# A two-layer diffusion backbone on one core: modulation passes placed anew, identity products in TensorE's waits, an earlier token copy and earlier expert loads

## The chip, the core and the metric

The kernel runs on one core of a Trainium2 chip. The metric is the device time of one execution in microseconds, as the median of several runs. All tensors are fp32. The engines are called by the names of the profile: PE (TensorE), DVE (VectorE), ACT (ScalarE), POOL (GpSimd) and SP (SyncE, which only issues transfers here).

## What is computed

Two layers (DEPTH 2) over 256 latent tokens and 256 context tokens of width 1024. The second layer returns the latent tokens only, so it works on half of the queries. Cut to what matters:

```python
for l in range(2):
    mod  = silu(c)     @ w_mod[l] + b_mod[l]      # 6 x 1024: shift, scale, gate, twice
    modc = silu(c_ctx) @ w_mod[l] + b_mod[l]      # the same for the context tokens
    h = rms_norm(x, norm1_g) * (1 + s1) + sh1     # hc likewise, with modc
    z = h @ w_in                                  # 1024 x 6144: four mixers and 4 x 1024 gates
    ya = differential_attention(z)                # "A": 4 heads of 32, two softmaxes
    yb = hyena_long_convolution(z)                # "B"
    yc = windowed_gqa(z)                          # "C": 4 heads of 64, 2 of keys
    yd = conformer_convolution(z)                 # "D"
    y  = sum(sigmoid(z_gate_i + b_gate_i) * (y_i @ w_branch[i]) for i in range(4)) @ w_out
    x  = x + g1 * y
    t  = rms_norm(x, norm2_g) * (1 + s2) + sh2
    x  = x + g2 * hier_moe(t)     # top group of 4, top 2 of its 4 experts: 16 experts of 1024x512
```

## The kernel before

Nothing in the order of work is left to a scheduler. `layer_order(l)` writes one list of steps, each a pair of an engine letter (T is PE, V is DVE, S is ACT, P is POOL) and a name such as `("br", 1, 2, 7)`. Each engine runs its own steps in the order of that list and waits on semaphores for the steps of others. `merge` and `spread` distribute one list evenly over another. The step names used below:

- `gate` (line 1163) is the product of the normed tokens with one eighth of a branch's gate columns, 16 PE instructions; `br` (line 1264) is a branch's output product. ACT, DVE and POOL turn both into the gated sum. The gates are the filler with which PE bridges the attentions' waits.
- Attention A is `qkTA` (line 1271), `sA` (1285), maxima on DVE (2398), exponentials on ACT (1800), `pTA` (1300) turned out by ACT (1810), `yA` (1311), its norm `yM` (1319), DVE's `yrA` and `ynA` (2441) and `yR` (1326). Attention C has `qkTC`, `sC` and `yC` (1278, 1293, 1336). `rsA` on DVE follows `ssA`, sums of squares (2364), and stands ahead of the rotation (2083 to 2103).
- `modv` (line 2180) is the adaLN modulation as DVE work: passes of 128x1024 over chunks of `wmod`. 120 of them are strewn over the stages, one column group (l, ch) at a time; 8 passes a group in layer 0, and 4 or 8 in layer 1. Two groups per layer run on PE instead (line 1116).
- `wo` (line 1347) is the output projection; then `xup` (2455, 2457), the second norm (`rstd`, `scale` at 2210, transposes at 1137), the router's logits (1366, 1372), `hb` (1377), `modB` (1129), `rank` (1385 to 1390), `slots`, `list` (1397) and, in layer 0, `sidelist` (1404), which build the lists of tokens of each expert. `rows` (2560 to 2584) works out row numbers for the later gathers.
- The experts run in pairs: tokens gathered by POOL (1975), turned on PE (1444, and 1449 for the side expert), copied out by DVE (2595, 2601), then up and gate products (1456, 1458) and down products (1466). In layer 1 the first tokens are made by a product (1578) instead of a gather.
- Between the layers stand `mod` and `modT` (1116, 1122) and the `mix` products (1356, 1357), which wait for the gathered expert results.

SP loads the weights in order of first use into a ring of six places of 1 MB (`plan_ring`, line 1064), and waits, ahead of a load, for the last reader of what lay there. Expert matrices are 2 MB and take two places; some go to buffers of other stages that are free by then (`load_early`, line 946, and lines 995, 1010, 1016), and later ones into places that the expert loop frees (957, 959). SP is one queue: a load behind one that waits is late too.

PSUM has 8 banks, which `plan_banks` gives out in rotation.

## Time and profile before

| | before |
|---|---|
| median of 3 runs | 1573.72 us (1573.6 to 1573.95) |
| the profiled execution | 1572.35 us, span 1570.6 us |
| PE busy | 1457.3 us, 93% of the span |
| DVE / ACT / POOL busy | 48% / 18% / 7% |
| chain that ended last | PE 79%, DVE 11%, DMA 3%, issue 3%, SP's queue 2%, ACT 2% |
| moved | 355.57 MB, mean 226 GB/s |
| granted PE clock, mean | 0.971 |

### The profile page before, as it was taken

The page shows a single profiled execution, that of the slowest core. Times are in us where ns is not written, and L with a number is a line of the kernel's source. Part 1 is how long each engine was busy: PE and PEld are TensorE (multiplying, and loading weights), DVE is VectorE, ACT ScalarE, POOL GpSimd, SP SyncE. Part 2 cuts the span into 40 slices and gives each one's busy share as a digit, 9 for nine tenths or more (in the row PEclk, how much of TensorE's full clock was granted, in tenths as well). Part 3 has the DMA queues.
Part 4 walks back from the last instruction along what each step waited for, and adds up shares of the span by engine and source line. Part 5 has one row for each costly group of instructions (what it writes and reads, how often), then busy time and mean ns, then how long its engine had stood idle before and what let it go on. Part 6 is the DMA issues. An engine that isn't in the chain of part 4 may idle for free.

```text
span 1570.6 us, 17267 instructions
## 1 busy us (share of the span) xinstructions
PE 1457.3 (93%) x6306; PEld 737.0 (47%) x6306; DVE 753.8 (48%) x1740; ACT 279.8 (18%) x579; POOL 114.0 (7%) x107
## 2 busy tenths in 40 slices
PE   6999999988899999699999998999879997999987
PEld 2544644443444444533333334865767874433332
DVE  4297676684565876511221214685887214211112
ACT  3201011421331200311111101111232202000000
POOL 0000011000111210000000001001001110000000
PEclk8999999998999999899999999999999998999999
DMA  9520243211324432799999976326534327999996
GB/s 374 198 79 31 77 158 137 81 54 53 108 81 145 174 142 68 294 351 405 415 407 418 409 318 258 138 81 240 219 123 168 114 75 311 424 418 422 422 421 244
DMA packets 49330, 355.57 MB, mean 226 GB/s; under 512 B 5568, under 2 KB 5952, under 8 KB 21984
## 3 DMA queue, kind: packets, MB, share of 16 engines
q1 hardware_dynamic: 41936, 330.79, 53.6%
q0 software_dynamic: 4016, 14.24, 2.4%
q10 hardware_dynamic: 3296, 9.44, 1.6%
q8 instruction: 53, 0.87, 0.2%
q14 instruction: 29, 0.24, 0.0%
HBM read 343.88 MB, written 10.56 MB: 226 GB/s over the span
## 4 chain that ended last, share of the span: by engine, by line
PE 79%; DVE 11%; DMA 3%; issue 3%; SPq 2%; ACT 2%; POOL 0%; DVEq 0%; ACTq 0%; POOLq 0%
PE ps L1163 25%; PE ps L1456 19%; PE ps L1176 6%; PE ps L1466 5%; PE ps L1347 5%; PE ps L1264 4%; SPq L946 2%; DVE n_ L2267 2%; DMA hT<-w 2%; PE ps L1137 1%; PE ps L1478 1%; DMA ring<-wmod 1%; PE ps L1300 1%; DVE mx L2398 1%; PE ps L1285 1%
## 5 line engine op out<-in xcount | busy, mean ns | idle before, releaser
L1163 PE MATMUL ps<-hT,ring 128*128 128x512 f32 (+1 forms) x1344 | 458.9, 497 | 4.5 <-ACT n_ L1800 3.0
L1163 PEld LDWEIGHTS ps<-hT,ring 128*128 128x128 f32 x1344 | 258.6, 195 | 180.2 <-issue 155.4
L1456 PE MATMUL ps<-ring,m 128*64 128x512 f32 x624 | 279.6, 600 | 10.3 <-ACT m L1883 3.5
L1456 PEld LDWEIGHTS ps<-ring,m 128*64 128x64 f32 x624 | 82.5, 138 | 184.7 <-issue 175.0
L2180 DVE SCALAR_TENSOR_TENSOR spare<-ring,crow 128x1024 bf16<-128x1024 f32 x120 | 154.1, 1284 | 4.1
L1176 PE MATMUL ps<-ring,hT 128*128 128x512 f32 (+1 forms) x352 | 125.1, 515 | 0.0
L1458 PE MATMUL ps<-n_,m 128*64 128x512 f32 x224 | 102.5, 607 | 0.0
L1264 PE MATMUL ps<-yT,ring 128*128 128x512 f32 (+1 forms) x256 | 95.9, 498 | 0.0
L1458 PE MATMUL ps<-wide,m 128*64 128x512 f32 x208 | 93.7, 597 | 0.0
L1176 PEld LDWEIGHTS ps<-ring,hT 128*128 128x128 f32 x352 | 66.7, 190 | 55.1 <-issue 51.4
L1458 PE MATMUL ps<-hT,m 128*64 128x512 f32 x208 | 91.9, 595 | 0.0
L1947 POOL TENSOR_TENSOR wide<-wide,gates 128x512 f32<-128x512 f32 (+1 forms) x48 | 61.8, 1287 | 411.9 <-DVE gates L2357 411.9
L1347 PE MATMUL ps<-ring,wide 128*128 128x512 f32 x192 | 83.1, 593 | 1.1 <-issue 1.1
L1759 ACT ACTIVATE gates<-ps,hbg 128x512 f32<-128x512 f32 (+1 forms) x64 | 37.1, 580 | 245.1 <-PE ps L1163 183.4
L2605 DVE SCALAR_TENSOR_TENSOR m<-m,ps 128x512 f32<-128x512 f32 x16 | 11.0, 687 | 142.9 <-ACT m L1869 142.9
L2267 DVE SCALAR_TENSOR_TENSOR n_<-n_,col 128x512 f32<-128x512 f32 (+1 forms) x120 | 74.2, 618 | 4.3
L2357 DVE SCALAR_TENSOR_TENSOR gates<-gates,ps 128x512 f32<-128x512 f32 (+1 forms) x48 | 26.6, 554 | 97.5 <-PE ps L1264 92.2
L2618 DVE TENSOR_TENSOR m<-m,ps 128x512 f32<-128x512 f32 x16 | 11.0, 687 | 106.0 <-PE ps L1458 106.0
L1264 PEld LDWEIGHTS ps<-yT,ring 128*128 128x128 f32 x256 | 46.1, 191 | 30.9 <-issue 24.8
L1466 PE MATMUL ps<-ring,yT 128*32 128x512 f32 x256 | 58.1, 595 | 0.0
L1347 PEld LDWEIGHTS ps<-ring,wide 128*128 128x128 f32 x192 | 36.2, 190 | 46.1 <-issue 46.1
L1975 POOL DMA_INDIRECT m<-h_scratch,m x15 | 14.2, 946 | 484.5 <-PE ps L1444 335.0
(362 smaller groups left out, 1710.9 us busy)
## 6 DMA issues: line engine op xcount, KB each, us to landing
ring<-w SPq DMA_DIRECT2D x39, 2048.0 KB, 11.4
ring<-win SPq DMA_DIRECT2D x52, 1024.0 KB, 5.1
ring<-wmod SPq DMA_DIRECT2D x48, 1024.0 KB, 5.1
n_<-w SPq DMA_DIRECT2D x13, 2048.0 KB
hT<-w SPq DMA_DIRECT2D x13, 2048.0 KB, 18.1
wide<-w SPq DMA_DIRECT2D x13, 2048.0 KB, 15.9
ring<-wbr SPq DMA_DIRECT2D x8, 1024.0 KB, 5.0
ring<-wout SPq DMA_DIRECT2D x8, 1024.0 KB, 5.1
```

Of the source, the lines that this page charges most:

```text
L946: sp.dma_start(ap, fourths(experts_weights[w][1, 2 * e + two][:, 512 * k:512 * (k + n)]))\
L1163: last = pe.matmul(b[:, 0:W], w[:, k, jj * P:(jj + 1) * P], hT[:, k, 0:W], start=(k == 0), stop=(k == KD - 1))
L1176: last = pe.matmul(b[:, 0:wid], hT[:, k, t * P:(t + 1) * P], chunk3(parts[k // ks], ks)[:, k % ks, 0:wid], start=(k == 0), stop=(k == KD - 1))
L1264: last = pe.matmul(b[:, 0:W], w[:, k, j * P:(j + 1) * P], yT[:, bi in (1, 2), k, 0:W], start=(k == 0), stop=(k == 1))
L1347: last = pe.matmul(b, acc[:, k, t * P:(t + 1) * P], chunk3(part_of, 4)[:, k % 4, :], start=(k == 0), stop=(k == KD - 1))
L1456: pe.matmul(ps[0:HALF, bnk, :], left[:, k, 0:HALF], even[k], start=(k == 0), stop=(k == n_k - 1), skip_group_check=True)
L1458: last = pe.matmul(ps[HALF:P, bnk, :], left[:, k, HALF:P], odd[k], start=(k == 0), stop=(k == n_k - 1), skip_group_check=True)
L1466: last = pe.matmul(ps[SIDE * g:SIDE * (g + 1), bnk, :], left[:, k0 + k, rows_:rows_ + SIDE], weights[:, k0 + k, cols_], start=(k == 0), st ...
L1759: last = act.activation(gth[:, g % 2, 0:W], bank(("gate", l, bi, j))[:, 0:W], ACT.Tanh, bias=hbg[:, bi * 8 + j:bi * 8 + j + 1], scale=0.5)
L1947: last = nc.gpsimd.tensor_tensor(acc[:, j, 0:W], acc[:, j, 0:W], gtmp[:, g % 2, 0:W], ALU.add)
L2180: last = v.scalar_tensor_tensor(out=spare[:, 0, :].bitcast(BF16), in0=chunk3(cn, 2)[:, block_ % 2, :], scalar=0.5, in1=crow[:, s, :], op0= ...
L2267: last = v.scalar_tensor_tensor(out=o, in0=ud[:, j, 0:ns, k:k + 256], scalar=w(k), in1=o, op0=ALU.mult, op1=ALU.add)
```

## The change

- **DVE's modulation passes.** In layer 0 group (0, 7) goes from attention A to attention C, and the groups behind it each move one stage on; three groups instead of two stand in the `wo` stage, four passes behind each of its first half tiles, and none behind the last two. In layer 1 groups 8 and 9 go from the conformer and rope stage to attention C, and 10 and 11 from attention A to the first half of the last gates. Ahead of each attention A, none stands behind the last three tiles of `zA`.
- **Identity products.** `busy` steps multiply the identity by itself, 128x128 by 128x512, into a bank that nobody reads: in layer 0 two ahead of `rank`, one behind `list`, three behind `sidelist`, and after the experts two ahead of `mod` and four ahead of the `mix`; in layer 1 five ahead of the second norm's last tile, three ahead of `rank` and one behind `list`.
- **Order in the router.** `modB` moves behind `rank`. In layer 0 the first copies of turned tokens (`firstturned`) move ahead of `rows`.
- **Loads.** `wout` comes in chunks of 2 MB that take two places. In layer 1, 4 MB of expert weights (`n_`, `m`, `con`, `mr`) are issued behind the last `yC`, ahead of the last gate weights and of `wout`; 4 MB more (`yT` and others, and the ring's `w1`) behind `br(1,2,7)`, where they stood behind the first `wo`.

```diff
@@ -258,6 +258,11 @@
     return net, spectrum
 
 
+def kept_busy(l, where, n):
+
+    return [("T", ("busy", l, where, n))] if n else []
+
+
 def norm_steps(l, n, tiles):
 
     out = [("S", ("sq", l, n, t)) for t in tiles]
@@ -352,15 +357,15 @@
 
     turned = lambda chunks: [[g] for c in chunks for g in modv_steps(*c)]
     if l == 0:
-        with_za, with_conformer, in_a, in_c = [(0, 4)], [(0, 5), (0, 6)], [(0, 7)], [(0, 8), (0, 9)]
-        behind, with_wo = [(0, 10), (0, 11), (1, 0), (1, 1)], [(1, 2), (1, 3)]
+        with_za, with_conformer, in_c = [(0, 4)], [(0, 5), (0, 6)], [(0, 7), (0, 8)]
+        behind, with_wo = [(0, 9), (0, 10), (0, 11), (1, 0)], [(1, 1), (1, 2), (1, 3)]
     else:
-        with_za, with_conformer, in_a, in_c, behind, with_wo = [(1, 6), (1, 7)], [(1, 8), (1, 9)], [(1, 10), (1, 11)], [], [], []
+        with_za, with_conformer, in_c, behind, with_wo = [(1, 6), (1, 7)], [], [(1, 8), (1, 9)], [(1, 10), (1, 11)], []
     za_groups = []
     for t in range(TILES):
         za_groups += [[("T", ("zAq", l, t)), ("S", ("zAqout", l, t))]] if t < tt else []
         za_groups += [[("T", ("zAk", l, t)), ("S", ("zAkout", l, t)), ("P", ("sqA", l, t)), ("V", ("ssA", l, t))]]
-    o += merge(za_groups, turned(with_za)) + [("V", ("rsA", l))]
+    o += merge(za_groups[:-3], turned(with_za)) + [s for g in za_groups[-3:] for s in g] + [("V", ("rsA", l))]
     projections = [[("P", ("sqC", l, t)), ("V", ("ssC", l, t))] for t in range(TILES)]
 
     def prepared(b):
@@ -402,12 +407,14 @@
     half = len(units) // 2
     turns = [g for g in prepared("C") if g[0][0] == "T"]
     ropes = [[("V", ("rsC", l))]] + [g for g in prepared("C") if g[0][0] == "V"]
-    o += settled(spread(conformer[12:] + spread(gate_groups(1, False), turned(in_a)),
+    o += settled(spread(conformer[12:] + gate_groups(1, False),
                         units[:half] + spread(units[half:], ropes) + turns))
     o += settled(spread(spread(gate_groups(0, False), turned(in_c)), attention("C")))
     net, spectrum = filter_groups(l + 1) if l + 1 < DEPTH else ([], [])
 
-    o += merge(spread(gate_groups(2, False), turned(behind)), net)
+    last_gates = gate_groups(2, False)
+    n = len(last_gates) if l == 0 else len(last_gates) // 2
+    o += merge(spread(last_gates[:n], turned(behind)) + last_gates[n:], net)
     o += gate_steps(l, (4, 5))
     for t in range(tt):
         for hf in range(2):
@@ -419,32 +426,39 @@
                 o += [("S", ("sq", l, 2, u)) for u in range(t)] + [("V", ("rstd", l, 2, 0, t))]
             o += [("V", ("xup", l, t, hf))]
             n, left = 2 * t + hf, turned(with_wo)
-            o += [s for g in left[n * len(left) // (2 * tt):(n + 1) * len(left) // (2 * tt)] for s in g]
+            o += [s for g in left[4 * n:4 * n + 4] for s in g]
     o += [g[0] for g in spectrum[1:]]
     o += [("V", ("scale", l, 2, t)) for t in range(tt - 1)]
     normed = norm_steps(l, 2, [tt - 1])
+    o += kept_busy(l, "norm", 0 if with_side(l) else 5)
     o += normed[:1] + [g[1] for g in spectrum[1:]] + normed[1:] + modulated_steps(l, 2)
     o += [("T", ("lg", l)), ("S", ("lgrow", l)), ("T", ("lgT", l)), ("V", ("lgout", l)), ("V", ("picks", l))]
     for t in range(tt):
         for hf in range(2):
             o += [("T", ("hb", l, t, hf)), ("S", ("hbout", l, t, hf))]
         o += [("S", ("hstore", l, t))]
-    o += gate_steps(l, (10, 11))
-    o += [("T", ("rank", l)), ("V", ("slots", l))]
+    o += kept_busy(l, "rank", 2 if with_side(l) else 3)
+    o += [("T", ("rank", l)), ("V", ("slots", l))] + gate_steps(l, (10, 11))
     if not with_side(l):
         o += [("V", ("firstrows", l))]
     o += [("T", ("list", l)), ("V", ("list", l))]
+    o += kept_busy(l, "list", 1)
     if with_side(l):
         o += [("V", ("sideslots", l)), ("T", ("sidelist", l)), ("V", ("sidelist", l))]
+        o += kept_busy(l, "sidelist", 3)
     o += [("V", ("weights1", l)), ("S", ("rexp", l)), ("V", ("weights2", l))]
     if not with_side(l):
         o += [("V", ("weighted", l))]
+    if with_side(l):
+        o += [("V", ("firstturned", l))]
     o += [("V", ("rows", l))]
     o += [("T", ("experts", l)), ("S", ("experts", l)), ("V", ("experts", l)), ("P", ("experts", l))]
     o += [("V", ("diag", l))] if with_side(l) else []
     if l + 1 < DEPTH:
         one, two = mod_steps(l + 1, [4]), mod_steps(l + 1, [5])
+        o += kept_busy(l, "boundary", 2)
         o += one[:2] + two[:2] + one[2:] + two[2:]
+        o += kept_busy(l, "gather", 4)
     if l + 1 < DEPTH:
         return o + boundary_steps(l)
     for t in range(tt):
@@ -474,7 +488,7 @@
     if kind == "br":
         return [("wbr", l, rest[0])]
     if kind == "wo":
-        return [("wout", l, rest[1], half) for half in range(2)]
+        return [("wout", l, rest[1])]
     if kind == "experts":
 
         return [("w1", l), ("w3", l), ("w2", l)]
@@ -488,7 +502,7 @@
 
 def places_of(chunk):
 
-    return 2 if chunk[0] in ("w1", "w3", "w2") else 1
+    return 2 if chunk[0] in ("w1", "w3", "w2", "wout") else 1
 
 
 def plan_ring():
@@ -521,6 +535,10 @@
 
 CHUNKS, PLACE, BEFORE = plan_ring()
 CHUNK_AT = {name: i for i, (name, _) in enumerate(CHUNKS)}
+ORDER_AT = {s: i for i, s in enumerate(ORDER)}
+BEHIND_SCORES = next(i for i, (name, _) in enumerate(CHUNKS) if name[1] == DEPTH - 1 and any(
+    ORDER_AT[CHUNKS[b][1]] > ORDER_AT["T", ("yC", DEPTH - 1, live(DEPTH - 1) - 1)] for b in BEFORE[i]))
+LAST_WOUT = ("wout", DEPTH - 1, 1)
 FIRST_WIN = {l: next(name for name, _ in CHUNKS if name[:2] == ("win", l)) for l in range(DEPTH)}
 
 
...
@@ -975,6 +995,10 @@
             sp.dma_start(col[:], cols).then_inc(params_landed, 16)
             sp.dma_start(row[:], rows).then_inc(params_landed, 16)
             for i, (name, _) in enumerate(CHUNKS):
+                if i == BEHIND_SCORES:
+                    sp.wait_ge(tensor_done, tensor("yC", 1, live(1) - 1))
+                    sp.dma_start(odd_at["w1"], w1[1, 1]).then_inc(odd_landed["w1"], 16)
+                    load_early(("w3", 0), ("w3", 1, 0), "attention")
                 for b in BEFORE[i]:
 
                     old, (engine, last) = CHUNKS[b]
@@ -990,15 +1014,9 @@
                     base = l * PAIRS
                     weights = experts_weights[name[0]]
                     sp.dma_start(place, weights[l, 0]).then_inc(here, 16)
-                    if name[0] == "w1":
+                    if name[0] == "w1" and not l:
                         sp.wait_ge(tensor_done, tensor("yC", l, live(l) - 1))
                         sp.dma_start(odd_at["w1"], w1[l, 1]).then_inc(odd_landed["w1"], 16)
-                        if l:
-                            load_early(("w3", 0), ("w3", 1, 0), "attention")
-                            sp.wait_ge(tensor_done, tensor("br", l, 2, KD - 1))
-                            sp.wait_ge(vector_done, vector(*mod_ready(l, 11)))
-                            load_early(("w1", 1), ("w1", 1, 1), "branches")
-                            load_early(("w3", 1), ("w3", 1, 1), "branches")
                     if name[0] != "w2":
                         continue
                     if l:
@@ -1057,11 +1075,16 @@
                 if name == FIRST_WIN[1]:
 
                     sp.wait_ge(y_gathered[live(0) - 1], 32)
-                if name[0] in ("wmod", "wout"):
+                if name[0] == "wmod":
                     src = source[name[0]][name[1], name[2]][:, PLACE_COLS * name[3]:PLACE_COLS * (name[3] + 1)]
                 else:
                     src = source[name[0]][name[1], name[2]]
                 sp.dma_start(place, src).then_inc(here, 16)
+                if name == LAST_WOUT:
+                    sp.wait_ge(tensor_done, tensor("br", 1, 2, KD - 1))
+                    sp.wait_ge(vector_done, vector(*mod_ready(1, 11)))
+                    load_early(("w1", 1), ("w1", 1, 1), "branches")
+                    load_early(("w3", 1), ("w3", 1, 1), "branches")
                 if name == ("wmod", 0, 0, 1):
                     sp.dma_start(x[:], xin).then_inc(x_landed, 16)
                 if name == ("wmod", 0, 2, 1):
@@ -1120,6 +1143,11 @@
                     pe.wait_ge(scalar_done, scalar("modrow", l, *rest))
                     for j in range(4):
                         last = pe.transpose(b[:, j * P:(j + 1) * P], mr[:, rest[0] % 2, j * P:(j + 1) * P], ident)
+                    last.then_inc(tensor_done, 1)
+                elif kind == "busy":
+                    _, n_products = rest
+                    for i in range(n_products):
+                        last = pe.matmul(b, ident, ident.unsqueeze(1).broadcast_to([P, 4, P]), start=True, stop=True)
                     last.then_inc(tensor_done, 1)
                 elif kind == "modB":
                     ch, v = rest
...
@@ -2556,6 +2595,10 @@
                     link(v.scalar_tensor_tensor(out=pw[:, 0, 0:tt], in0=p2, scalar=0.5, in1=total, op0=ALU.mult, op1=ALU.mult))
                     last = v.tensor_tensor(pw[:, 1, 0:tt], pw[:, 0, 0:tt], rtmp[:, 9, 0:tt], ALU.mult)
                     last.then_inc(vector_done, 1)
+                elif kind == "firstturned":
+                    turned(l, 0)
+                    side_turned_out(0)
+                    v.nop().then_inc(vector_done, 1)
                 elif kind == "rows":
                     link(v.tensor_copy(tok, c("token")))
```

What stands in DVE's row in layer 1's attention A before: maxima (2398), softmax weights (2420 to 2423), rotation of C (2083 to 2103), a gate (2357), and two passes (2180).

```order
L2180 SCALAR_TENSOR_TENSOR spare,mod<-ring,crow 128x1024
L2398 TENSOR_REDUCE mx<-ps 128x1 x2
L2399 TENSOR_SCALAR nm<-mx 128x2
L2420 RECIPROCAL rr<-sums 128x2
L2421 TENSOR_TENSOR nlam<-rr,nlam 128x1
L2422 TENSOR_SCALAR n_<-n_,rr 128x512
L2423 SCALAR_TENSOR_TENSOR n_<-n_,nlam 128x512
L2083 TENSOR_TENSOR m<-m,rsc 128x128
L2085 TENSOR_TENSOR m<-m,row 128x128
L2096 TENSOR_TENSOR n_<-m,con 128x128
L2100 TENSOR_TENSOR n_<-m,con 128x4x16 x2
L2103 TENSOR_TENSOR m<-n_ 128x128
```

The same place of the change; its line numbers are 39 higher (2437 for 2398, 2122 for 2083, and a pass would be 2219).

```order
L2437 TENSOR_REDUCE mx<-ps 128x1 x2
L2438 TENSOR_SCALAR nm<-mx 128x2
L2459 RECIPROCAL rr<-sums 128x2
L2460 TENSOR_TENSOR nlam<-rr,nlam 128x1
L2461 TENSOR_SCALAR n_<-n_,rr 128x512
L2462 SCALAR_TENSOR_TENSOR n_<-n_,nlam 128x512
L2122 TENSOR_TENSOR m<-m,rsc 128x128
L2124 TENSOR_TENSOR m<-m,row 128x128
L2135 TENSOR_TENSOR n_<-m,con 128x128
L2139 TENSOR_TENSOR n_<-m,con 128x4x16 x2
L2142 TENSOR_TENSOR m<-n_ 128x128
L2486 SCALAR_TENSOR_TENSOR yT<-n_,col,ps 128x2x128
```

The passes before the maxima and behind the branch product are gone; the first one that follows stands behind attention C's first maxima.

PE's row in layer 0's router before: `hb` (1377), `modB` (1129), `rank` (1385 to 1390), `list` (1397), `sidelist` (1404) and the turning of the tokens (1444).

```order
L1377 MATMUL ps<-con,hT 128x128 x32
L1129 MATMUL ps<-con,mod 128x128 x16
L1385 MATMUL ps<-m,con 128x80
L1388 MATMUL ps<-m,con 128x48
L1388 MATMUL ps<-m,con 128x32
L1388 MATMUL ps<-m,con 128x16
L1390 MATMUL ps<-m,con 128x80
L1397 MATMUL ps<-m 128x16 x8
L1404 MATMUL ps<-m 64x16 x8
L1444 MATMUL ps<-con,m 128x128 x8
```

The same place of the change, with the identity products at line 1150 and `modB` at 1157.

```order
L1404 MATMUL ps<-con,hT 128x128 x32
L1150 MATMUL ps<-con 128x512 x2
L1412 MATMUL ps<-m,con 128x80
L1415 MATMUL ps<-m,con 128x48
L1415 MATMUL ps<-m,con 128x32
L1415 MATMUL ps<-m,con 128x16
L1417 MATMUL ps<-m,con 128x80
L1157 MATMUL ps<-con,mod 128x128 x16
L1424 MATMUL ps<-m 128x16 x8
L1150 MATMUL ps<-con 128x512
L1431 MATMUL ps<-m 64x16 x8
L1150 MATMUL ps<-con 128x512 x3
```

The two identity products stand where `modB` stood, `modB` is behind `rank`, and three products lie between `sidelist` and the turning of the gathered tokens.

SP's queue in layer 1 before, from the last gate weights (`win`) to the early expert loads.

```order
L1064 DMA ring<-win 128x2048 x3
L1064 DMA ring<-wout 128x2048 x4
L992 DMA ring<-w 128x4096
L995 DMA n_<-w 128x4096
L946 DMA m<-w 128x1536
L946 DMA con<-w 128x1024
L946 DMA con<-w 128x512
L946 DMA m<-w 128x512
L946 DMA mr<-w 128x512
```

The same loads of the change (line 1000 for 995, 966 for 946, 1082 for 1064).

```order
L1082 DMA ring<-wmod 128x2048
L1000 DMA n_<-w 128x4096
L966 DMA m<-w 128x1536
L966 DMA con<-w 128x1024
L966 DMA con<-w 128x512
L966 DMA m<-w 128x512
L966 DMA mr<-w 128x512
L1082 DMA ring<-wmod 128x2048
L1082 DMA ring<-win 128x2048 x2
L1082 DMA ring<-wout 128x4096 x2
L966 DMA yT<-w 128x2048
```

Six expert loads, 4 MB, now stand ahead of the last `wmod` chunk, of the last two `win` chunks and of `wout`.

## Rows read from the trace of the kernel before

**Rows 1.** First line of the profile page: the span.

```profile
span 1570.6 us, 17267 instructions
```

**Rows 2.** Windows: PE, PEld, DVE, ACT, POOL busy us (instructions), PEclk, DMA share, GB/s.

```profile
300.00:402.00 102.00, 88.86 (x314) 43.60 (x312) 67.52 (x197) 25.25 (x69) 10.07 (x7) 0.93 0.21 73
1098.00:1202.00 104.00, 88.90 (x461) 72.39 (x459) 83.93 (x212) 27.96 (x67) 9.69 (x10) 0.92 0.47 172
1202.00:1246.00 44.00, 43.13 (x251) 34.60 (x252) 20.95 (x64) 16.63 (x41) 5.78 (x8) 1.00 0.37 135
1246.00:1282.00 36.00, 36.00 (x180) 31.59 (x175) 3.39 (x9) 4.17 (x9) 5.06 (x7) 1.00 0.34 119
...
1350.00:1560.00 210.00, 197.56 (x882) 71.78 (x878) 25.56 (x47) 17.18 (x30) 5.62 (x6) 1.00 0.98 405
```

**Rows 3.** Windows of line 2180 alone: DVE busy us (instructions), PEclk, DMA share.

```profile
300.00:402.00 102.00, 9.87 (x16) 0.93 0.21 73
1098.00:1202.00 104.00, 19.97 (x32) 0.92 0.47 172
```

**Rows 4.** Timeline of PE, layer 0, attention A.

```profile
335.58 7.03 PE L1163 MATMUL ps<-hT,ring 128*128 128x512 f32 x16
...
350.72 9.23 PE L1163 MATMUL ps<-hT,ring 128*128 128x512 f32 x16
...
388.51 0.41 PE L1326 MATMUL ps<-con,n_ 128*128 128x128 f32 x2 [2.92 <-DVE n_ L2441]
```

**Rows 5.** Timeline of PE, layer 1, attention A.

```profile
1103.39 1.09 PE L1271 MATMUL ps<-con,m 128*128 128x128 f32 x4 [4.92 <-DVE m L2103]
1104.28 6.12 PE L1163 MATMUL ps<-hT,ring 128*128 128x256 f32 x16
...
1111.54 3.62 PE L1163 MATMUL ps<-hT,ring 128*128 128x256 f32 x16
```

**Rows 6.** Timeline of DVE ahead of layer 1's attention A.

```profile
1091.86 1.57 DVE L2180 SCALAR_TENSOR_TENSOR spare<-ring,crow 128x1024 bf16<-128x1024 f32 x1
...
1095.29 0.19 DVE L2379 TENSOR_SCALAR small<-ssa 128x64 f32<-128x64 f32 x1
```

**Rows 7.** Timeline of PE, layer 0, norm 2 and router.

```profile
633.11 6.74 PE L1137 MATMUL ps<-n_,x 128*128 128x128 f32 x58 [2.14 <-DVE n_ L2210]
...
662.13 1.94 PE L1444 MATMUL ps<-con,m 128*128 128x128 f32 x8 [2.62 <-DMA m<-h_scratch,m]
664.01 1.11 PE L1449 MATMUL ps<-con,yT 64*128 64x64 f32 x8
667.44 1.11 PE L1456 MATMUL ps<-ring,m 128*64 128x512 f32 x1 [2.32 <-DVE m L2595]
```

**Rows 8.** Timeline of DVE, layer 0, end of the router.

```profile
661.82 0.17 DVE L2560 CAST m<-con 128x4 uint32<-128x4 f32 x1
...
666.70 0.69 DVE L2595 COPY m<-ps 128x512 f32<-128x512 f32 x1
```

**Rows 9.** Windows: the same columns as in rows 2, end of layer 0's router.

```profile
660.00:670.00 10.00, 5.54 (x22) 3.26 (x24) 6.56 (x33) 0.91 (x3) 2.77 (x3) 0.50 0.68 252
```

**Rows 10.** Timeline of PE between the layers.

```profile
958.39 1.30 PE L1356 MATMUL ps<-wide,n_ 128*128 128x512 f32 x2 [3.44 <-DMA hT<-y_scratch,m]
```

**Rows 11.** Timeline of PE, layer 1, norm 2 and first tokens.

```profile
1316.13 5.90 PE L1137 MATMUL ps<-n_,x 128*128 128x128 f32 x30 [3.07 <-DVE n_ L2210]
...
1335.53 6.63 PE L1578 MATMUL ps<-m,wide 128*128 128x128 f32 x32 [1.08 <-DVE m L2526]
```

**Rows 12.** Timeline of DVE, layer 1, copy of the first tokens.

```profile
1342.25 0.69 DVE L2595 COPY m<-ps 128x512 f32<-128x512 f32 x1 [1.84 <-PE ps L1578]
```

**Rows 13.** Timeline of SP's queue, layer 1: expert loads and the first refill.

```profile
1303.83 0.33 SPq L992 DMA_DIRECT2D ring<-w  x1
...
1350.13 0.33 SPq L959 DMA_DIRECT2D ring<-w  x1
```

**Rows 14.** Timeline of PE, layer 1's experts.

```profile
1503.33 0.61 PE L1456 MATMUL ps<-x,m 128*64 128x512 f32 x1 [3.05 <-DMA gates<-w]
```

More of the change, by code:

```diff
@@ L1343, in _ @@
                     pe.wait_ge(pool_done, pool("gadd", l, 2, KD - 1))
+                    use(("wout", l, half))
+                    w = chunk3(("wout", l, half))
                     for k in range(KD):
-                        part_of = ("wout", l, half, k // 4)
-                        use(part_of)
-                        last = pe.matmul(b, acc[:, k, t * P:(t + 1) * P], chunk3(part_of, 4)[:, k % 4, :],
-                                         start=(k == 0), stop=(k == KD - 1))
+                        last = pe.matmul(b, acc[:, k, t * P:(t + 1) * P], w[:, k, :], start=(k == 0), stop=(k == KD - 1))
                     last.then_inc(tensor_done, 1)
@@ L2672, in pair @@
                             side_result(e)
-                    turned(0)
-                    if side:
-                        side_turned_out(0)
-                    else:
+                    if not side:
+                        turned(l, 0)
                         v.wait_ge(rows_weighed, 1)
```

24 lines of the change are left out of this document (13 added, 11 removed).

## Prediction

> **What bounds the kernel.** The page first: the span is 1570.6 us [rows 1], and the profiled execution took 1572.35 us, 1.4 us less than the median of the runs. PE is busy 93% of the span, so the gain must come from PE's idle time or from the clock that it is granted. The windows say where both lie. In layer 0's attention A PE works 88.86 of 102.00 us at a granted clock of 0.93, in layer 1's 88.90 of 104.00 at 0.92, while DVE is busy for 67.52 and 83.93 us; the 44 us behind it (attention C) hold only 0.9 us of idle PE, and the last gates (1246 to 1282) none at all: 36.00 of 36.00 us at full clock, DVE busy 3.39 us [rows 2]. Layer 1's experts move 405 GB/s at a DMA share of 0.98 [rows 2]: there the transfers set the pace, and PE is seen waiting for one for 3.05 us [rows 14]. The timelines of PE and DVE then say what ends each wait.
>
> **Attention A, layer 0.** PE waits 13.1 us (102.00 less 88.86). Behind each longer wait it runs at half speed for a while: the same 16 gate instructions take 7.03 us when it was busy and 9.23 us behind a wait [rows 4]. A mean of 0.93 [rows 2] means 14% of 102 us at the lower of the two levels (1.2 and not 2.4 GHz), some 14 us, which costs at most half of it, 7.1 us; I take 6. So 19 us are at stake. The change takes 8 passes out, 9.87 us of DVE time [rows 3]. They are no sum to subtract: a pass of 1.2 us costs only where it stands ahead of a maximum, a softmax weight or the norm `ynA`, for which PE waits (2.92 us [rows 4]). More gates also go into the waits for `yR`. The ends: 3 us if only a third of the passes stood on the path, 17 if nearly all waits and their clock go. Some latencies (exponentials on ACT, turning on ACT) stay without passes. I take **8**.
>
> **Attention A, layer 1.** PE waits 15.1 us and the clock of 0.92 costs at most 8.3, of which I take 6 (a group of 16 gates took 6.12 us behind the wait of 4.92 us, and 3.62 later [rows 5]). Out go 16 passes, 19.97 us of DVE's 83.93 [rows 2, 3]; DVE is nearer to being the bound here than in layer 0. Ahead of it, two passes stood between the last `ssA` and `rsA`: from 1091.86 to 1095.29, 3.4 us [rows 6], on the path to the 4.92 us wait on DVE [rows 5]. These 3.4 us come in nearly whole. Together **13**, between 6 and 20.
>
> **Where the passes go.** In layer 1, 8 go to attention C: 10 us more on a DVE busy 20.95 of 44 us beside a PE without idle time [rows 2]: cost 1, between 0 and 3, the upper end if three passes stand right ahead of a maximum. 8 go to the last gates, 10 us on a DVE busy 3.39 of 36: nothing, since PE's gates cover them; without that cover each costs 1.25 us (19.97 through 16 [rows 3]). In layer 0 eight more stand in the `wo` stage ahead of the last two half tiles, under output products: nothing. Behind the last two `xup` none is left, where one pair (2.5 us by the same price) held DVE ahead of the wait of 2.14 us [rows 7]: gain **2**, between 0 and 2.6.
>
> **Start of layer 0's experts.** Tokens are turned by 664.07 and the side tokens by 665.12, but DVE works on `rows` from 661.82 on and copies only at 666.70; PE starts at 667.44 after 2.32 us [rows 7, 8]. With the copy first, it is done in 0.7 us from 664.1, and PE starts as its turning ends at 665.1: 2.3 us. `rows` then runs under the first products. The clock in this window is 0.50 [rows 9]: turning at 1.94 us for 8 would take about half, of which 0.9 us are on the path, and the first five steps of the experts (1.11 against about half) would give 2.5 us if PE was kept at 2.4 GHz. An identity product is two instructions of 128x512, as a gate is 16: 7.03 through 16 makes 0.44 each [rows 4], so 0.88 us a product, and 1.76 at the lower level. Three behind `sidelist` end 2.6 to 5.3 us after it, while PE waited for the gathered tokens 2.62 us and more: warm they fit, cold they hold up the turning by up to 2.5 us. Sum **5**, between -2.5 and 6.5. The Trainium skill bears on this ("TensorE: Matmul & The Clock Gate", Part 4): a transpose in PE's transpose mode does not count as PE-busy in the same way and does not engage the full clock. By that rule the turning itself would lose again what the identity products kept, and the sum here would be 2.5 less. The trace shows 58 norm transposes in 6.74 us in layer 0 and 30 in 5.90 us in layer 1 [rows 7, 11], so transposes run at either level; what sets the level no row decides. I give the 2.5 us less a chance of 0.4, within this term's bounds.
>
> **Between the layers.** Six products, 5.3 us at full clock, in waits of 2.4 us ahead of `mod` and 3.44 us ahead of the `mix` [rows 10]. The four ahead of the `mix` take 3.5 us warm: they end when the transfer lands or up to 1.7 us later, since the two ahead of `mod` run cold. The first `mix` products then run warm, 1.8 us less. **0**, between -3 and +1.
>
> **Layer 1, norm 2 and router.** Thirty transposes took 5.90 us behind a wait of 3.07, against 58 in 6.74 in layer 0 [rows 7, 11]: warm they take 3.5, but are paced by DVE's copies, so 1.8. The first tokens' product, 6.63 us at a low clock [rows 11], would take some 3.7; its copy at 1342.25 waited 1.84 us for it [rows 12], and DVE's own work ahead of the copy limits the gain to these 1.8. With 0.4 for `modB` in the wait for `slots`: **4**, between 1 and 5.
>
> **Loads in layer 1.** SP came to the expert weights at 1303.83 [rows 13], after a stretch in which nothing moved. From 1350.13, the first refill, the schedule still asks for 38 matrices of 2.097 MB and 7 gathers of 0.524 MB: 83.4 MB. The window from 1350 moved 405 times 210, 85.0 MB [rows 2]. So only 1.6 MB of the early loads was still owed at the first refill: 3.9 us at 413 GB/s (405 through 0.98). Loading 8 MB earlier brings at most that much to the experts, which stay bound by DMA; it gives **3.8**, between 0 and 7, the upper end if all PE waits such as [rows 14] go. What is won before the experts is kept, because the refills start with PE's first expert, not by the clock.
>
> The loads have a price ahead of them. 4.2 MB go into SP's queue before the last `wmod`, two `win` chunks and `wout`. One branch's gates are eight channels in 36 us [rows 2], 4.5 us each, and a `win` chunk serves two. The third of the stage, the first one behind the expert loads, is needed 18 us after `yC`. Ahead of it are 4.2 MB of expert weights and up to 5 MB of ring chunks, estimated: 9.2 MB at 0.413 MB/us are 22 us, from a start some 4 us before `yC`'s end. It lands at 18 us, so on the edge: I take a stall of **-2**, between -5 and 0. The Trainium skill says ("DMA: Bandwidth & Descriptors", Queues, rings and completion order) that SP's transfers share one ring on each of the 16 engines, consumed in ring order. By that rule none of the later chunks overtakes; without it the gate weights would share the bandwidth and the stall would still be 2 to 5. The trace's windows do not show the two side by side.
>
> **Sum.** 8 + 13 - 1 + 2 + 5 + 0 + 4 + 3.8 - 2 = 32.8 us. 1572.35 - 32.8 = 1539.6, and 1.4 more for the median: **1541 us**.
>
> **Rivals.**
> (a) The passes carry their stall along (0.20). In attention C or the last gates they delay `ropeC`'s, `mxC`'s or the gates' own DVE work, and the waits in attention A were latency of the chain DVE, ACT, PE, not passes. For it: 8 of 16 passes go into a stage where PE waits for maxima; part of A's waits name ACT. Against it: PE has 0.9 us of idle in C, DVE half of its time [rows 2]. Both attentions then give only 5 and C costs 3: 18 less, **1559 us**.
> (b) Identity products on the path (0.06), the other side. 21 products cost 0.88 us each warm and 1.76 cold, 18 to 37 us, if PE's waits were not there, because the releaser itself waits for PE (banks in rotation, `modB` behind `rank`). It becomes slower than before only from where more than 33 us are lost, so every product must run cold and in the way, or half of them beside (a): **1578 us**. Against it: waits of 2.32, 2.62, 3.07 and 3.44 us end on DVE or on a transfer [rows 7, 10, 11].
> (c) SP's queue starves the last gates (0.06): all of the 9.2 MB late and `wout` behind it too, 10 us of stall (4.2 MB through 0.413) in place of 2: **1549 us**, inside the forecast's range.
> (d) Nearly all waits go (0.13): 17 and 20 in the attentions and 7 in the experts: 19 more, **1522 us**; I expect from it half at most, 1530.
> The forecast itself has 0.55, with 1532 to 1552 as its own range.
>
> **How the numbers follow.** What a measurement of this kernel can tell from no change is about 0.2%, 3.1 us. The range of 8 in 10 takes in (c), half of (d) and most of (a): 1526 to 1561. Faster: the forecast, (c), (d) and (a), but for the tail of (a) in which the experts' early loads give nothing either: 0.91. Within 0.2%: 0.04. Slower: 0.05, of (b).
>
> **What the changed profile would show.** Right: idle PE in the two attentions under 10 us each and a clock above 0.95; no pass between the last `ssA` and `rsA`; the first copy of turned tokens ahead of `rows` in layer 0, and PE's first expert product within 1 us of the turning; the window of the router's end well above 0.50; PE's wait for a transfer in the last gates under 3 us; layer 1's experts shorter by 4 us from the first refill on. Wrong: waits on `win` of over 5 us in the last gates, maxima of C late behind passes, identity products that end after the step behind them was ready, or a token turning that still runs at half speed.

## The result and the profile after

The changed kernel takes 1557.19 us in the median of 6 runs (1554.92 to 1561.74), against 1573.12 us before. The ratio is 0.9904, 95% interval 0.9893 to 0.9916: 16 us faster, where 33 were forecast. As a time it lies inside the prediction's range of 1526 to 1561; the gain is about half of the forecast one. Its runs spread over 6.8 us; the six of the kernel before spread over 1.6, and its runs beside the experiments over 3.1, 5.7 and 4.9. The profiled execution is one of the slower ones: 1559.5 us, span 1557.8 us.

The first line of the changed kernel's page, and the page's row of the modulation passes:

```profile
span 1557.8 us, 17344 instructions
...
L2219 DVE SCALAR_TENSOR_TENSOR spare<-ring,crow 128x1024 bf16<-128x1024 f32 x120 | 155.3, 1295 | 9.0 <-DMA ring<-wmod 4.9
```

The passes take what they took, 1.3 us each; ahead of them DVE now stands idle for 9.0 us in all, 4.9 of them for `wmod` chunks.

The changed kernel's windows (PE, PEld, DVE, ACT, POOL busy, clock, DMA share, GB/s): both attentions A, ten microseconds at a time in the last gates of layer 1, the experts of layer 1 and the end of layer 0's router.

```profile
300.00:402.00 102.00, 88.48 (x317) 42.51 (x317) 56.32 (x179) 25.21 (x70) 10.36 (x8) 0.93 0.15 52
1098.00:1202.00 104.00, 96.16 (x507) 76.57 (x506) 64.64 (x183) 33.17 (x81) 10.98 (x13) 0.97 0.32 112
1235.00:1245.00 10.00, 10.00 (x49) 8.79 (x48) 6.73 (x11) 1.42 (x3) 3.39 (x2) 1.00 1.01 423
1245.00:1255.00 10.00, 5.00 (x22) 4.10 (x21) 4.80 (x9) 0.47 (x1) 3.11 (x2) 0.92 1.04 424
1255.00:1265.00 10.00, 10.00 (x37) 8.28 (x35) 0.72 (x2) 0.47 (x1) 1.00 (x2) 0.74 0.47 195
1350.00:1550.00 200.00, 190.17 (x830) 68.89 (x827) 23.34 (x43) 16.10 (x28) 4.68 (x5) 0.99 0.95 393
660.00:670.00 10.00, 9.78 (x61) 3.98 (x63) 5.53 (x26) 1.19 (x2) 1.84 (x2) 1.00 0.92 355
```

Read against [rows 2], the first row is the surprise: DVE has 11 us less to do in layer 0's attention A, and PE's 13.5 us of idle time and its clock of 0.93 are what they were. The last row is the opposite case: the clock of 0.50 [rows 9] is now 1.00. The windows of the last gates show a PE idle for 5 us beside a DMA share of 1.04, where it had no idle time before.

Windows at fixed times cut shifted stages at different places, so the rest goes by milestones on PE's timeline, the first or the last row of a line. Stages that are alike in both are left out. Lengths in us:

| stage, from PE's timeline | before | changed | forecast gain | gain |
|---|---|---|---|---|
| layer 0, A's turned queries to C's first scores | 178.9 | 177.9 | 8 | 1.0 |
| layer 0, C's first scores to last `yC` | 90.1 | 88.4 | 0 | 1.7 |
| layer 0, first `wo` to the norm's last transposes | 71.6 | 70.1 | 2 | 1.5 |
| layer 0, `rank` to the end of the up products | 292.0 | 287.8 | 5 | 4.3 |
| from there to the last `mix` between the layers | 31.1 | 29.8 | 0 | 1.3 |
| from there to layer 1's turned queries | 130.2 | 127.7 | 3.4, in the 13 | 2.5 |
| layer 1, turned queries to C's first scores | 98.6 | 95.2 | 9.6, in the 13 | 3.3 |
| layer 1, C's first scores to last `yC` | 44.6 | 44.9 | -1 | -0.3 |
| layer 1, last `yC` to first `wo` | 36.3 | 44.5 | -2 | -8.2 |
| layer 1, end of `wo` to the first expert product | 32.4 | 27.3 | 4 | 5.1 |
| layer 1, first to last up product | 217.4 | 216.4 | 3.8 | 1.0 |

These gains and 0.4 us lost ahead of the first stage are 12.8 us, as the spans have it (1570.6 less 1557.8).

The last gates on the changed kernel's PE timeline:

```profile
1244.77 3.62 PE L1191 MATMUL ps<-hT,ring 128*128 128x256 f32 x16
1248.23 1.03 PE L1292 MATMUL ps<-yT,ring 128*128 128x256 f32 x4
1254.25 6.59 PE L1191 MATMUL ps<-hT,ring 128*128 128x256 f32 x16 [5.00 <-issue]
1260.68 1.03 PE L1292 MATMUL ps<-yT,ring 128*128 128x256 f32 x4
```

The wait is named "issue", a wait for nothing that the profile names; SP's queue and the load's time to landing say what it was.

```profile
1231.07 0.33 SPq L1082 DMA_DIRECT2D ring<-wmod  x1
1231.82 0.33 SPq L1000 DMA_DIRECT2D n_<-w  x1
...
1235.58 0.45 SPq L966 DMA_DIRECT2D mr<-w  x1
1238.22 0.33 SPq L1082 DMA_DIRECT2D ring<-wmod  x1
1239.79 4.05 SPq L1082 DMA_DIRECT2D ring<-win  x2
```

The DMA view of 1215 to 1280 on the `win` chunks, where 13.1 is the median of three, and that of 1239.6 to 1240.2, which holds the one issued at 1239.79 alone:

```profile
ring<-win SPq DMA_DIRECT2D x3, 1024.0 KB, 13.1
ring<-win SPq DMA_DIRECT2D x1, 1024.0 KB, 14.4
```

In the median of the whole kernel a `win` chunk lands 4.9 us after its issue; this one took 14.4, and 1239.79 plus 14.4 is 1254.2, when PE's stall ends. After it the same gates take 6.59 us and not 3.62. So the stall cost 5.0 and the clock another 3.0.

### The profile page after: what moved, and what is told of

Read it like the earlier page. It is cut to its first block and busy times, and to the rows that moved or that the text cites. A ratio compares the mean times of both kernels' runs of the same rounds, so it can differ in the third digit from the quotient of the medians.

```text
span 1557.8 us, 17344 instructions
## 1 busy us (share of the span) xinstructions
PE 1464.1 (94%) x6348; PEld 733.9 (47%) x6348; DVE 756.3 (49%) x1740; ACT 279.8 (18%) x579; POOL 119.0 (8%) x107
## 5 line engine op out<-in xcount | busy, mean ns | idle before, releaser
L1974 POOL TENSOR_TENSOR wide<-wide,gates 128x512 f32<-128x512 f32 (+1 forms) x48 | 69.7, 1452 | 407.7 <-DVE gates L2396 407.7
```

The lines of the kernel that those rows point to most:

```text
L1974: last = nc.gpsimd.tensor_tensor(acc[:, j, 0:W], acc[:, j, 0:W], gtmp[:, g % 2, 0:W], ALU.add)
```

## The experiments

**1 and 2. Where the loads stand.** The changed kernel, with the first 4 MB of the expert loads behind the last gate weights (the first edit, below), or with the code of the early loads as it was before the change (the second), where all of them stand behind `wout`:

```diff
-BEHIND_SCORES = next(i for i, (name, _) in enumerate(CHUNKS) if name[1] == DEPTH - 1 and any(
-    ORDER_AT[CHUNKS[b][1]] > ORDER_AT["T", ("yC", DEPTH - 1, live(DEPTH - 1) - 1)] for b in BEFORE[i]))
+BEHIND_SCORES = next(i for i, (name, _) in enumerate(CHUNKS) if name == ("wout", DEPTH - 1, 0))
```

> The changed kernel with the first group of early expert loads (4.2 MB) issued behind the last gate weights and ahead of the output weights. Theory Q (the queue starves the gates): the 44.5 us from the end of layer 1's last yC to the first output product come back to 36 to 37 us, PE's wait of 5.0 us inside the last gates and the half-speed product behind it are gone, and nothing is lost elsewhere, since the expert loads still land before layer 1's experts: 7 to 8 us faster than the changed kernel, about 1549 us. Rival D (DVE and the passes moved into the last gates hold them up): the stage stays at 43 to 45 us and the time at 1557.

> The changed kernel with all early expert loads back behind the first output product, as before. Theory Q: the last gates take 36 to 37 us (8 us won), but layer 1's experts owe the transfers again what the early loads brought. If the experts are bound by transfers as I priced it, they give back 3 to 4 us: about 1553 us. If the early loads are worth nothing there: 1549 us. If they are worth all that they move (8 MB, 19 us): 1568 us.

Measured: 1551.02 us (ratio 0.986, 0.9845 to 0.9875) and 1553.86 us (0.9882, 0.9866 to 0.9897). In both the last gates take 36.3 us again. PE's timeline of experiment 1 in that stage has no wait until the first `wo`:

```profile
1249.51 3.62 PE L1190 MATMUL ps<-hT,ring 128*128 128x256 f32 x16
1252.96 1.03 PE L1291 MATMUL ps<-yT,ring 128*128 128x256 f32 x4
1253.82 3.62 PE L1190 MATMUL ps<-hT,ring 128*128 128x256 f32 x16
...
1268.53 1.96 PE L1374 MATMUL ps<-ring,wide 128*128 128x512 f32 x4 [0.72 <-issue]
```

In experiment 1 the `win` chunk issued at 1240.20 landed after 7.0 us. The queue was the cause. Both kernels have the passes in that stage too, and it takes what it took before the change, so they cost nothing there.

Experiment 2 is not as late as the kernel before. Its `wout` still comes in chunks of 2 MB, and SP comes to the expert loads at 1267.05, 64 us ahead of the first refill; before the change it was 46 us, and it is 87 in experiment 1 and 107 in the changed kernel. From the first refill (1331.61 and 1331.48) to the last product that waits for a matrix (1513.71 and 1512.78) experiments 1 and 2 take 182.1 and 181.3 us; it was 183.3 before, and 180.6 in the changed kernel. So 4 MB moved by 23 us did not lengthen this stretch. Whether the 2.8 us between the two medians are more than the spread stays open; their intervals overlap. In the two profiles the second kernel is longer at two places at which only the clock differs, by 1.7 us each: layer 0's attention C, and the products behind the last wait for a matrix, of which the last section tells.

**3. No identity products.**

```diff
-    return [("T", ("busy", l, where, n))] if n else []
+    return [("T", ("busy", l, where, n))] if n and (False) else []
```

> The changed kernel without any identity product. If they hold the clock up as I priced them, it loses some 2.5 us at the start of layer 0's experts, 1.8 in layer 1's norm, 2 to 3 in layer 1's first tokens and gets about 1 us back between the layers: 5 to 8 us slower than the changed kernel, about 1564 us. Rival: the order alone (modB, the token copy) gives the gain and the products are idle work: within 2 us of the changed kernel, or faster by up to 3.

Measured: 1568.07 us in 8 runs (ratio 0.9974, 0.9963 to 0.9984), 11 us slower than the changed kernel, where I had expected 5 to 8. The stages that hold such products give 8.8 us of it: `rank` to the end of layer 0's up products 289.8 and not 287.8 us, up products to last `mix` 31.2 and not 29.8, end of layer 1's `wo` to its first expert product 32.7 and not 27.3. The experts of layer 1 are 1.0 longer. Stages without these products differ too: layer 1's attention A by 0.6 and layer 0's attention C by 1.7 longer, layer 0's attention A by 1.4 shorter. Without them, at the end of layer 0's router, PE's timeline reads:

```profile
658.14 1.94 PE L1471 MATMUL ps<-con,m 128*128 128x128 f32 x8 [2.66 <-DMA m<-h_scratch,m]
660.22 1.11 PE L1476 MATMUL ps<-con,yT 64*128 64x64 f32 x8
661.27 1.11 PE L1483 MATMUL ps<-ring,m 128*64 128x512 f32 x1
```

And in the changed kernel:

```profile
655.42 4.79 PE L1150 MATMUL ps<-con 128*128 128x512 f32 x6
660.05 1.04 PE L1471 MATMUL ps<-con,m 128*128 128x128 f32 x8
661.02 0.71 PE L1476 MATMUL ps<-con,yT 64*128 64x64 f32 x8
661.94 0.64 PE L1483 MATMUL ps<-ring,m 128*64 128x512 f32 x1 [0.22 <-DVE m L2091]
```

Three products, two PE instructions each, began at the low clock and took 4.79 us, and the turning comes 1.9 us later for them. Behind them everything runs at the high clock, and the up products are 2.6 us shorter in all.

**4. Layer 0's attention A in its old order, without the passes.** The passes are put in where they stood, so that the gates fall as before, and are then left out of the stage:

```diff
+    marks = turned([(0, 7)] if l == 0 else [(1, 10), (1, 11)])
+    if l == 0:
+        stage = settled(spread(conformer[12:] + spread(gate_groups(1, False), marks),
+                               units[:half] + spread(units[half:], ropes) + turns))
+        o += [s for s in stage if s[1][0] != "modv" or s[1][2] not in (7,)]
...
```

> The changed kernel, with every engine's order in layer 0's attention A as it was before the change but without the eight modulation passes, which stay where the change put them. Theory O (the passes were worth something, but taking them out of the list shifted the gates away from PE's waits, which cost as much): the stage from the first turned queries of A to the first scores of C gets 3 to 8 us shorter than in the changed kernel and than before, total 1549 to 1554. Rival P (the passes never stood on the path; the waits are latency of scores, softmax and turning): the stage is as long as before within 1.5 us and the total stays at 1556 to 1558.

Measured: 1557.91 us (0.9908, 0.9893 to 0.9923), the changed kernel's time; but the stage takes 172.8 us, 5.1 less. The changed kernel's PE timeline at the first two `yR` (L1354), the second with the next turning of softmax weights (L1328) close behind:

```profile
304.41 0.66 PE L1354 MATMUL ps<-con,n_ 128*128 128x128 f32 x2 [3.55 <-DVE n_ L2480]
...
330.63 0.42 PE L1328 MATMUL ps<-con,m 128*128 128x128 f32 x2
330.88 1.88 PE L1292 MATMUL ps<-yT,ring 128*128 128x512 f32 x4
333.70 0.41 PE L1354 MATMUL ps<-con,n_ 128*128 128x128 f32 x2 [0.93 <-DVE n_ L2480]
339.45 0.69 PE L1328 MATMUL ps<-con,n_ 128*128 128x128 f32 x2 [5.35 <-ACT m L1827]
```

In the old order a gate group stands between `yM` and `yR` at both places, and `yR` (L1360 in this experiment) waits for nothing:

```profile
301.27 7.03 PE L1197 MATMUL ps<-hT,ring 128*128 128x512 f32 x16
308.14 0.38 PE L1360 MATMUL ps<-con,n_ 128*128 128x128 f32 x2
...
324.73 7.03 PE L1197 MATMUL ps<-hT,ring 128*128 128x512 f32 x16
331.59 0.38 PE L1360 MATMUL ps<-con,n_ 128*128 128x128 f32 x2
```

The longest waits that this experiment keeps there, without any pass in the stage:

```profile
345.72 1.09 PE L1345 MATMUL ps<-n_,m 128*64 128x128 f32 x16 [1.63 <-ACT n_ L1843]
...
360.67 8.74 PE L1197 MATMUL ps<-hT,ring 128*128 128x512 f32 x16 [3.04 <-ACT n_ L1833]
...
383.81 0.41 PE L1360 MATMUL ps<-con,n_ 128*128 128x128 f32 x2 [2.92 <-DVE n_ L2486]
```

The 2.92 us are those of before, to the hundredth [rows 4], and so are the 3.04:

```profile
365.37 8.74 PE L1163 MATMUL ps<-hT,ring 128*128 128x512 f32 x16 [3.04 <-ACT n_ L1800]
```

In this profile the 5.1 us were partly given back where the code is alike: C 90.1 us and not 88.4, and layer 1's router and first tokens 2.0 us longer. The last gates were 2.0 us shorter. No median shows the 5.1 us by itself.

**8. The fourth corner: new order, passes put back.**

```diff
-        with_za, with_conformer, in_c = [(0, 4)], [(0, 5), (0, 6)], [(0, 7), (0, 8)]
+        with_za, with_conformer, in_c = [(0, 4)], [(0, 5), (0, 6)], [(0, 8)]
...
+        marked = settled(spread(conformer[12:] + spread(gate_groups(1, False), turned([(0, 7)])),
+                                units[:half] + spread(units[half:], ropes) + turns))
+        for at, s in enumerate(marked):
+            if s[1][0] == "modv" and s[1][2] == 7:
+                stage.insert(at, s)
...
```

> The changed kernel with the eight passes put back into layer 0's attention A at the places in the list that they had, everything else there in the changed order: the fourth corner beside before (old order with passes, 178.9 us), the changed kernel (new order without, 176.5 to 177.9) and the old order without (172.8). If passes and order cost independently: 177.9 plus 6, so 183 to 184 us for the stage. If the shifted gates hide the passes (one wait takes the other's place): 178 to 180.

One run, 1561.14 us; the stage 180.4 us, its longest wait

```profile
341.03 0.69 PE L1335 MATMUL ps<-con,n_ 128*128 128x128 f32 x2 [6.62 <-ACT m L1834]
```

So the passes cost 6.1 us in the old order (178.9 against 172.8) and 2.5 to 3.9 in the new one (180.4 against 177.9, or 176.5 in the second and third experiments). It is as if one wait partly hid the other: the stage lies 0.4 us above the upper end of my second case, and far below the first. All these numbers are of single profiles. The old order without passes has seven: 172.4 to 172.8 us in six, and 169.1 in the tenth experiment's, where the waits are the same and PE's clock is not.

**5, 6 and 7. Put together.** The first edit and the fourth's; the same with layer 1's attention A in its old order without passes; the fifth with one identity product behind the side list.

```diff
-        o += kept_busy(l, "sidelist", 3)
+        o += kept_busy(l, "sidelist", 1)
```

> Early expert loads behind the last gate weights and, in layer 0's attention A, the order of before without the passes: the two edits of the first runs together. If stages add up: layer 0's attention A 172.8 us from its first turned queries to C's first scores (177.9 in the changed kernel), last gates 36.3 us (44.5), so 1545 to 1547 us. If the second run of the order (no faster in its median than the changed kernel, though 5.1 us shorter in its stage) shows that a gain there is given back by the clock later, the median stays at 1550 to 1551.

> The same, and layer 1's attention A too in the order of before without its eight passes. The stage from turned queries to C's first scores took 98.6 us before and 95.2 to 95.8 with the change. Theory O (the shifted gates cost there too): 90 to 93 us and 3 to 5 us faster than the kernel without this edit. Rival P (layer 1's waits are latency of the exponentials and of PSUM banks; neither passes nor places of gates matter much): 94.5 to 96.5 us, same time within 1.5.

> The first of these kernels with one identity product behind the side list in place of three. Three delay the turning of the tokens by 1.9 to 2.3 us (4.6 to 5.0 us from the side list's end to the turning, 2.7 without any). If one keeps the clock up as well as three: turning 2.7 us behind the side list, PE at full speed in the first expert products, 2 us faster. If the clock needs all three: turning at 2.7 but the products at half speed, 2.5 us given back, so no gain or 0.5 slower.

Measured: 1547.13 us (0.9839, 0.9823 to 0.9855), 1546.4 us (0.9837, 0.982 to 0.9855) and 1548.39 us (0.9847, 0.9827 to 0.9867). The fifth kernel beats the changed one by 10 us, and its interval lies clear of the changed kernel's. Its stages hold both gains, 172.8 and 36.3 us. Its median is 4 us under that of experiment 1, the loads' edit alone, but their intervals overlap. In the sixth, layer 1's stage takes 94.3 us, and 93.1 in the fifth; the same code as in the fifth took 95.2 to 95.8 in the changed kernel and in experiments 1 to 4, so no effect of the order is to be seen there. In the seventh the turning starts 2.7 us behind the side list, but at the low clock, and the up products take 273.4 us and not 272.2: what it wins is given back, as its second case had it (`rank` to the end of the up products 288.2 us, 288.0 in the fifth).

**9. DVE's chain for C ahead of A's maxima.** The fifth kernel, and:

```diff
-    ropes = [[("V", ("rsC", l))]] + [g for g in prepared("C") if g[0][0] == "V"]
+    ropes = [g for g in prepared("C") if g[0][0] == "V"]
+    o += [("V", ("rsC", l))]
```

> The kernel of gates_and_order (1547.1 us), with rsC, DVE's chain of 12 small operations (2.6 us) for attention C, ahead of attention A's first maxima instead of in the middle of them. In the changed kernel layer 1's scores of the fourth head are ready at 1143, but DVE comes to their maxima only at 1152.22, behind yrA and rsC, and PE waits 3.4 us for the exponential behind it. Theory S (what is left of the waits is DVE's own small chains, not passes): layer 1's stage goes from 93.1 to 95.8 us down to 90 to 92, layer 0's from 172.8 to 171 or less: 2 to 5 us faster. Rival P (latency of one head's chain over ACT and PE): both stages the same within 0.5 us but for the clock, time 1546 to 1548.

A miss: 1551.19 us (0.9843, 0.9823 to 0.9863, which is the fifth's ratio), layer 1's stage 97.0 us, layer 0's 172.4. The wait behind the exponential shrank from 3.4 to 2.6 us only, and new ones of 2.0 and 2.9 us came; behind the first of these `yA` ran at the low clock, 3.61 us for 1.97.

**10. Layer 1's passes back in attention A.** The fifth kernel, and:

```diff
-        with_za, with_conformer, in_c, behind, with_wo = [(1, 6), (1, 7)], [], [(1, 8), (1, 9)], [(1, 10), (1, 11)], []
+        with_za, with_conformer, in_c, behind, with_wo = [(1, 6), (1, 7)], [], [(1, 8), (1, 9)], [], []
...
+        o += settled(spread(conformer[12:] + spread(gate_groups(1, False), marks),
+                            units[:half] + spread(units[half:], ropes) + turns))
```

> The kernel of gates_and_order with the eight passes of layer 1's groups 10 and 11 back in attention A at the places they had. The stage took 98.6 us before and takes 93.1 to 95.8 without. If these passes made the difference: 97 to 99 us and 3 to 5 us slower. If it came from the passes ahead of the stage (conformer and rope stage) or from the clock: 94 to 96 us, same time within 1.5.

The stage takes 98.1 us (98.6 before the change), with the wait of before, 5.09 us for the same exponential. The kernel before and this one:

```profile
1169.95 0.69 PE L1326 MATMUL ps<-con,n_ 128*128 128x128 f32 x2 [5.09 <-ACT n_ L1800]
1149.12 0.69 PE L1359 MATMUL ps<-con,n_ 128*128 128x128 f32 x2 [5.09 <-ACT n_ L1832]
```

So these eight passes are what the stage had to gain: 3.7 us against the sixth (same order), 5.0 against the fifth, and 2.3 to 2.9 against the profiles of 95.2 to 95.8. The median, 1548.38 us in 4 runs (0.9856, 0.9826 to 0.9886), has too wide an interval to show it.

**11. Two identity products in layer 0's attention C.** The fifth kernel, and:

```diff
+    first = next(i for i, s in enumerate(stage) if s[0] == "T" and s[1][0] == "pTC")
+    o += stage[:first] + kept_busy(l, "scores", 0 if l else 2) + stage[first:]
```

> The kernel of gates_and_order with two identity products in the wait of 2.4 us for the first exponentials of layer 0's attention C. The stage from C's first scores to its last product came out in the profiles either at 88.4 us or at 90.1, in kernels that are alike there: behind the same wait of 2.4 us the next 16 gates took 7.0 or 8.7 us. Theory K (a wait of about 2.4 us is where the clock may or may not fall, and products in it settle it): always 88.4, and 1 to 2 us faster in the median, with a narrower spread. Rival: 90.1, or the same time.

C took 88.4 us, and the gates behind the wait 7.03 us, but the `wo` stage 59.4 us where it had been 57.5 to 57.9: 112 of its products took 50.0 us and not 48.3, behind a wait of 0.6 us for a `wout` chunk. Whether the one brought the other is not shown. 1548.09 us (0.9836, 0.9822 to 0.9849): no gain.

## Why the prediction was wrong

The signs of the terms were right. Four of them came out worse than priced, and they make up 23 us of gain that did not come. Two more fell short by 1.2 us together, three gave 3.1 more than priced, and layer 0's attention C gave 1.7, by the clock, which no term held.

- **"More gates also go into the waits for `yR`"** is the step that failed in layer 0 (8 forecast, 1.0 measured). Taking eight entries out of an evenly spread list moved the gates too, and at the first two heads' `yR` they left the wait. The new order of PE's steps could have been read for this, and I priced the removal alone. The passes were worth 6.1 us (178.9 less 172.8), of which the shift took 5.1 back (177.9 less 172.8). With the passes in, the shift costs 1.5 (180.4 less 178.9).
- **"A stall of -2, between -5 and 0"** (measured -8.2). The queue's bytes were about right. I counted on 4 us of transfers done before `yC`'s end; but the queue was not empty then: chunks issued from 1227.28 on were still under way at `yC`'s end (1231.8), the next `win` chunk among them, which itself took 8.1 us. The gate weights landed 22 us behind `yC` and not 18. And PE, having waited 5.0 us, paid 3.0 more at the low clock, which the term left out (1.5 and 2.7 in experiments 4 and 8, behind waits of 4.4 and 4.6 us at the same place). The Trainium skill's rule on the ring ("DMA: Bandwidth & Descriptors", Queues, rings and completion order) is that on each of the 16 engines SP's descriptors are consumed in ring order. The trace agrees: the `win` chunk took 14.4 us behind 4.2 MB of expert loads, and 7.0 in experiment 1, where they stood behind it.
- **Layer 1's attention A, 13** (5.8 measured, up to 8.0 in profiles of the same code there). With no pass ahead of `rsA`, the wait of 4.92 us [rows 5] became 2.43, a gain of 2.5 us where I took 3.4. The passes within the stage are worth 3.7 us in the same order, and 2.3 to 5.0 against the new one; I took 9.6 for them, six tenths of the other waits and the clock there (10.2 and 6). The rest is not theirs, and what it is stays partly open: the chain for C, moved away, did not free it.
- **The experts' 3.8** (1.0). They are bound by transfers from the first refill, as reasoned, and from there to the last matrix 2.7 us were won (183.3 to 180.6). That all of it is the backlog is not shown: experiment 2, with the loads 42 us later against the refill, has 181.3. The other 1.7 went where the last products, behind a wait of 2.6 us, ran at the low clock, as they had not before: 1.06 us for one instead of 0.6.

Right were the norm's passes (2.4 us, for 2; the stage has a net 1.5, since `wo` lost 0.9, and 0.75 of that is a wait for the second `wout` chunk, which is 2 MB now), the token copy and the clock at the start of layer 0's experts, and layer 1's norm and router. The identity products were underpriced, 11 us in the medians where I expected 5 to 8.

The Trainium skill's rule that the full clock does not engage for a transpose in PE's transpose mode ("TensorE: Matmul & The Clock Gate", Part 4) had put 2.5 us in doubt. For this kernel's transposes the traces do not bear it out; whether they use that mode no run shows. Behind the identity products the turning and the products behind it both ran at the high clock, 1.04 us for 1.94, 0.64 for 1.11. The kernel before already decided the question that I left open: its 58 norm transposes in layer 0 ran at a granted clock of 1.00 throughout, and in layer 1 the mean was 0.59 over 30 of them behind a wait, and 1.00 after them. Its windows:

```profile
633.20:639.80 6.60, 6.60 (x58) 6.46 (x58) 3.21 (x8) 3.81 (x8) 0.00 (x0) 1.00 1.00 427
1316.20:1322.00 5.80, 5.80 (x30) 5.64 (x30) 1.87 (x5) 2.01 (x4) 0.00 (x0) 0.59 1.03 369
1322.00:1326.00 4.00, 2.55 (x30) 1.97 (x30) 1.34 (x7) 1.13 (x3) 0.00 (x0) 1.00 1.06 430
```

Rival (a) came within 2 us in its time, 1559, and by luck: its attentions' 5 us are near the 6.8 measured, but it had C lose 3 us, where C gained 1.4 in all, and nothing of the last gates' 8.2. Half of its mechanism is there: waits of 3.04 and 2.92 us in layer 0 stayed without any pass. The other half is not: the passes carried no stall along; gates lost their place. Rival (c), at a chance of 0.06, was the mechanism of the last gates; only `wout`, which it had late too, came in time.

## What to carry to other kernels

Where work is spread evenly over a list, removing one kind of item moves all others: read the new order at each wait that the old one filled, and try the removal with the old places kept. A load that may come early still has to stand behind the loads that are needed first; count its bytes from the moment at which the queue is really empty, and add the time at the low clock behind any stall. A gain in one stage has to be read in that stage, and in several profiles, when runs of one kernel spread by as much as the gain; where two profiles differ, compare their waits first, and then what the same products took behind them.

## What was not expected of the hardware

A wait of 2.4 to 3.4 us on PE sometimes costs a low clock behind it and sometimes not, in the same code and behind the same wait. In layer 0's attention A, experiments 5 and 10 have the same order of work and, up to here, the same waits within 0.05 us; 16 gates took

```profile
360.81 8.54 PE L1196 MATMUL ps<-hT,ring 128*128 128x512 f32 x16 [3.04 <-ACT n_ L1832]
```

in the fifth, and in the tenth

```profile
359.26 7.13 PE L1196 MATMUL ps<-hT,ring 128*128 128x512 f32 x16 [3.04 <-ACT n_ L1832]
```

With two more such places the stage took 172.8 and 169.1 us. Three more stretches show the same:

- Layer 0's attention C, behind a wait of 2.42 us: 88.4 us (the changed kernel, experiments 1 and 10) or 90.1 (before, experiments 2 to 7 and 9).
- Layer 1's attention A in the changed order, behind a wait of 3.4 us: 95.2 to 95.8 us (the changed kernel, experiments 1 to 4) or 93.1 (5, 7, 8 and 11); the next four output products took 2.07 or 1.13 us.
- Layer 1's last expert products, behind a wait of 2.6 us: 31.5 us to the end (before, experiments 1, 9 and 10) or 33.2 (the changed kernel, experiments 2, 3, 5 to 7 and 11); 31.9 and 32.2 in experiments 8 and 4.

So a difference of 1.5 to 4 us between single profiles can be of the clock alone, and experiment 11 did not settle it. This is the likely source of the spread of 5 to 7 us between runs of one kernel; that it is, was not shown.
